# Combining the even layer's experts by matrix products with diagonal gates

## The chip, the cores and the metric

The kernel runs on one core of one Trainium2 chip. The metric is the device time of one execution in microseconds (us). Three runs of the kernel before gave 1182.02, 1181.76 and 1177.32 us; the median is 1181.76.

## What is computed

The reference is two consecutive layers of a hybrid backbone over 256 latent tokens and 256 context tokens of width 1024. Each layer has a mixer (the first, even one: state-space heads beside attention; the second, odd one: a matrix memory called mLSTM) and then a mixture of 16 experts, of which each token uses two. The change touches the end of the first layer's mixture and the beginning of the second layer:

```python
out = out + gates[..., e:e + 1] * (a @ w2[e])          # in moe: two of the 16 gates of a token are not zero
...
x_lat = x_lat + g_f * moe(h_lat, ...)                  # end of layer 0, latent stream
x_ctx = x_ctx + cg_f * moe(h_ctx, ...)                 # end of layer 0, context stream
...
h_lat = rmsnorm(x_lat, norm_mix[l]) * (1.0 + sc_m) + sh_m    # beginning of layer 1
h_ctx = rmsnorm(x_ctx, norm_mix[l]) * (1.0 + csc_m) + csh_m
```

So for each token the two expert outputs y0 and y1 are weighted by the token's two gates w0 and w1, the sum is multiplied by a row vector g, and the product is added to the residual stream x. Then x is normalised and modulated for the second layer.

## The kernel before, in words

The 512 tokens lie in four tiles of 128 (partitions are tokens): tiles 0 and 1 are the context (`CTX`), tiles 2 and 3 the latent stream (`LAT`). Each engine runs one hand-written list of steps in order (lines 2831 to 3012); semaphores tie the lists together, and a wait holds up everything behind it on its engine.

At the end of the first layer's mixture, GpSimd scatters expert outputs into a DRAM buffer (`ydram`), so that each token's two outputs lie side by side. When all are stored, SyncE issues four loads of 1 MB (line 2781) in the order tile 2, 3, 0, 1; each brings y0 and y1 of one tile into `ybuf(0, t)` and `ybuf(1, t)`. Behind these loads the same queue fetches the odd layer's input weights.

Meanwhile TensorE (PE) turns the modulation vectors g into rows (`pe_grow`, line 1312) and works out two chunks of the second layer's modulation (`COMB_MODS`: `pe_mod`, lines 423 and 429, with a copy by ScalarE at line 440 and a sum by VectorE at line 446).

The combination before is done by ScalarE and VectorE (DVE), tile by tile: ScalarE (ACT) scales y0 by w0 (`act_gate`, line 2792); VectorE takes y1 times w1 plus that (line 2799), times g (line 2800), plus x (line 2801). Then follows the normalisation: ScalarE sums the squares (line 512), VectorE and ScalarE work out the reciprocal root (lines 488 to 499), VectorE scales the tile (line 579), TensorE transposes it block by block (line 606), and ScalarE and VectorE write the modulated blocks out of PSUM into `hT` (lines 555 and 588).

The two latent tiles go first. Once their blocks of `hT` are written, TensorE starts the odd layer's input projection (`pe_in_odd`, line 1431). Its blocks are, in order, four query blocks that need only the latent half of `hT` (256 columns), then keys and values, which need both halves (512 columns). While the query blocks run, VectorE and ScalarE combine and normalise the context tiles. Before query block 3 TensorE transposes the context tiles (line 1448), and after it come the gates (`pe_gates`, line 673), which are the first product that needs the context's half of `hT`. An f32 product is written as one call of `pe.matmul` in the code and shows as two MATMUL instructions in the trace: eight calls of a query block are sixteen instructions.

Of the kernel before, what the change touches and what calls it, by code (L numbers as in the profile page):

```python
# [21 lines left out]
ACT = mybir.ActivationFunctionType  # L22
# [33 lines left out]
def lat(t):  # L56
    return t >= 2
# [7 lines left out]
def hybrid_program(nc, x, c, ctx, c_ctx, router_w, router_b, norm_mix, norm_ffn, w_mod, b_mod,  # L65
# [6 lines left out]
    def S(name):  # L72
        if name not in sems:
            sems[name] = nc.alloc_semaphore(name)
        return sems[name]
# [136 lines left out]
    def bank(b, n=512):  # L212
        return psum[:, b, 0:n]
# [76 lines left out]
    def dve_step(ins):  # L290

        ins.then_inc(S("dve_step"), 1)
        dve.wait_ge(*dve_more("dve_step"))
# [138 lines left out]
    def pe_mod(m):  # L432
        pe_mod_rows(m)
        pe_mod_cols(m)
# [61 lines left out]
    def act_rstd(n, a=0):  # L496
        v, y = stat2[:, 0, a:a + n], stat2[:, 1, a:a + n]
        act.wait_ge(*act_more("var_ready"))
        act.activation(y, v, ACT.Sqrt).then_inc(S("rstd_guess"), 1)
# [11 lines left out]
    def act_norm_sum(l, which, t):  # L511
        act.activation(turned_rows(l, which, t), xres[:, t, :], ACT.Square, accum_out=stat[:, t:t + 1]).then_inc(S("sum_ready"), 1)
# [918 lines left out]
    def pe_in_odd():  # L1431
        def transposes(j):
            kind, b = IN_ODD[j]
            pe.wait_ge(S("conv_done"), 6 + j + 1)
            bk = 4 + j % 2
            if j >= 6:
                pe.wait_ge(*pe_more("tok_done"))
            src = kTo[:, b, :] if kind == "k" else accv[:, j % 4, :]
            for t in range(NT):
                mm = pe.transpose(psum[:, bk, P * t:P * t + P], src[:, P * t:P * t + P], ident)  # L1440
            mm.then_inc(S("tok_full"), 1)

        at = None
        for j, (kind, b) in enumerate(IN_ODD):
            bk = (j + 2) % 4
            if j == 3:
                pe.wait_ge(S("mcol_done"), COMB_MODS[1] + 1)
                pe_norm_part(1, 0, CTX)
            if j == 4:
                pe_norm_end()  # L1450
                weights_here(OD0 + 1)
                w = slot(OD0 + 1, 32)
                pe_gates(6, [(w, H * q) for q in range(4)], (range(KD), range(KD))).then_inc(S("in_full"), 2)
            if j >= 4:
                pe.wait_ge(*pe_more("raw_ready"))
            pos = OD0 + 1 + j // 4 if j >= 4 else OD0
            if pos != at:
                weights_here(pos)
                at = pos
            w = slot(pos, 512)  # L1460
            tok = slice(STREAM, TOK) if kind == "q" else slice(0, TOK)
            for k in range(KD):
                mm = pe.matmul(bank(bk, tok.stop - tok.start), w[:, k, P * (b % 4):P * (b % 4) + P], hT[:, k, tok],  # L1463
                               start=k == 0, stop=k == KD - 1)
            mm.then_inc(S("in_full"), 1)
            if j >= 7:
                transposes(j - 3)
        for n in range(4):
            half, t = n // 2, 2 + n % 2
            pos = OD0 + 5 + half  # L1470
            if n % 2 == 0:
                weights_here(pos)
            pe.wait_ge(*pe_more("raw_ready"))
            w = slot(pos, 512)
            for k in range(KD):
                mm = pe.matmul(bank((18 + n) % 4), hT[:, k, P * t:P * t + P], w[:, k, :], start=k == 0, stop=k == KD - 1)  # L1476
            mm.then_inc(S("in_full"), 1)
            if n < 3:
                transposes(13 + n)
            if n == 2:  # L1480
                pe_ml_prepare()
        pe_ml_scores(3)
# [1191 lines left out]
    def ybuf(j, i):  # L2674
        return view(9216 + 1024 * (2 * i + j), [D])
# [111 lines left out]
        for half in ydram[1].rearrange("(h p a) n -> h p (a n)", h=2, p=P):  # L2787
            pool.dma_start(half, xres[:, 2:4, :].rearrange("p t n -> p (t n)")).then_inc(S("dram_zeroed"), 16)

    def act_gate(i):  # L2790
        act.wait_ge(*act_more(f"yback{i}", 16))
        act.activation(ybuf(0, i), ybuf(0, i), ACT.Copy, scale=gatew[:, i, 0:1]).then_inc(S("y1_scaled"), 1)

    def dve_combine(t):
        dve.wait_ge(S("grow_done"), GROW_AFTER[0][1])
        dve.wait_ge(*dve_more(f"yback{t}", 16))
        dve.wait_ge(*dve_more("y1_scaled"))
        y = ybuf(0, t)
        dve_step(dve.scalar_tensor_tensor(y, ybuf(1, t), gatew[:, t, 1:2], y, ALU.mult, ALU.add))
        dve_step(dve.tensor_tensor(y, y, grow_comb[0 if lat(t) else 1], ALU.mult))  # L2800
        dve.tensor_tensor(xres[:, t, :], xres[:, t, :], y, ALU.add).then_inc(S("comb_done"), 1)

    def act_combine():

        act_gate(2)
        act_gate(3)
        act_fetch(ACT.Sqrt)
        for n, t in enumerate(LAT):
            act.wait_ge(S("comb_done"), n + 1)
            act_norm_sum(1, 0, t)  # L2810
            act_rstd(1, t)
            act_gate(n)
        act_norm_rows(1, 0, 0)

    def dve_combine_all():

        for t in LAT:
            dve_combine(t)
        for t in LAT:
            dve_norm_scale(1, 0, [t])  # L2820
        dve_norm_rows(1, 0, 0)
        dve_odd_clear()
        for t in CTX:
            dve_combine(t)
        dve_norm_scale(1, 0, CTX)
        dve_norm_rows(1, 0, 1)

# [3 lines left out]
    with nc.Block() as block:  # L2831
# [41 lines left out]
        @block.scalar  # L2873
        def _(eng):
            act_setup()
            act_first_sums()
            act_mod(0)
            act_mod(1)
            act_first_rows(0)
            act_mod(2)  # L2880
            act_mod(3)
            act_first_rows(1)
            act.wait_ge(*act_more("raw_cleared"))
            act_in_even("xbc")
            act_setup_rest()
            act_conv()
            act_ssd_rows()
            act_in_even("kv", "q")
            act_rstd(10 * NT)
            act_in_even("z")  # L2890
            act_ssd_prepare()
            act_ssd()
            act_ssd_out()
            act_att_prepare()
            act_att()
            act_grow((0, 1), grow_out)
            act_out(0)
            act_router(0, ALL)
            act_moe(0)
            act_extra(0, ALL)  # L2900
            act.wait_ge(S("out_done"), 8)
            act_grow((0, 1), grow_comb)
            act_mod(COMB_MODS[0])
            act_mod(COMB_MODS[1])
            act_combine()
            act_in_odd()
            act_ml()
            act_ml_out()
            act.wait_ge(S("comb_done"), NT)
            act_grow((0,), grow_out)  # L2910
            act_out(1)
            act_router(1, LAT)
            act_moe(1)
            act_extra(1, LAT)

        @block.vector
        def _(eng):
            dve_setup()
            dve_norm_scale(0, 0, ALL)
            dve_mod(0)  # L2920
            dve_setup_rest()
            dve_mod(1)
            dve_first_bias(0)
            dve_first_acol(0)
            dve_first_rows(0)
            dve_mod(2)
            dve_mod(3)
            dve_first_bias(1)
            dve_first_acol(1)
            dve_first_rows(1)  # L2930
            dve_router_setup()
            dve_in_even()
            dve_ssd_rows()
            dve_qk_norm()
            dve_ssd_prepare()
            dve_ssd()
            dve_ssd_out()
            dve_att_prepare()
            dve_att()
            dve_mod_bias(0, FIRST, MODC)  # L2940
            dve_acol(0, 1)
            dve_out(0)
            dve_mod(NORM_MOD)
            dve_norm_rows(0, 1, 0)
            dve_mod(LIST_MODS[0])
            dve_router(0, ALL)
            dve_moe(0)
            dve_extra(0, ALL)
            dve_mod_bias(1, 0, 4)
            dve_acol(1, 0)  # L2950
            dve_mod(COMB_MODS[0])
            dve_mod(COMB_MODS[1])
            dve_combine_all()
            dve_mod_bias(1, 4, 8)
            dve_in_odd()
            dve_ml_prepare()
            dve_ml()
            dve_ml_out(OUT_ORDER[1])
            dve_mod_bias(1, 8, 10)
            dve_acol(1, 1)  # L2960
            dve_out(1)
            dve_norm_rows(1, 1, 0)
            dve_router(1, LAT)
            dve_moe(1)
            dve_last()
            dve_extra(1, LAT)

        @block.tensor
        def _(eng):
# [24 lines left out]
            pe_moe(0)  # L2994
            pe_extra(0, ALL)
            pe_grow(0, 1, (0, 1))
            for m in COMB_MODS:
                pe_mod(m)
            for t in LAT:
                pe_norm_part(1, 0, [t])  # L3000
            pe_norm_end()
# [85 lines left out]
```

## Time and profile before

| | |
|---|---|
| median of three runs | 1181.76 us (1177.32 to 1182.02) |
| the profiled execution's own time | 1179.53 us |
| its span, first to last instruction | 1177.9 us |
| TensorE busy | 1056.8 us |
| VectorE busy | 492.6 us |
| ScalarE busy | 257.6 us |
| mean granted TensorE clock | 0.967 of full speed |

The span is what the trace shows; the own time has 1.6 us more around it. Times in the trace count from the start of the span. The chain that ended last, followed back from the last instruction, is 73% TensorE and 11% VectorE. The stretch that the change touches lies between 638 and 690 us. Here a row of the timeline reads: start, duration, engine, line, operation, output<-input, shape, number of instructions merged, and in brackets the engine's idle time before it with what ended that.

### The profile page before, as it was taken

How to read it: one execution, taken by the hardware profiler on the slowest of the kernel's cores; microseconds unless marked ns; L12 is line 12 of the kernel's file. 1: busy time of each engine (PE TensorE's matmuls, PEld its weight loads, DVE VectorE, ACT ScalarE, POOL GpSimd, SP SyncE). 2: the span in 40 equal slices, each digit the busy share in tenths (PEclk: the TensorE clock that was granted, in tenths of full speed). 3: DMA queues.
4: the chain of work that ended last, by engine and by line, in shares of the span. 5: the costliest groups of instructions: out<-in, count | busy, mean ns of one | idle time of the engine just before them, and what ended most of it. 6: DMA issues, size and time to landing. Idle time of an engine off the chain costs nothing.

```text
span 1177.9 us, 14048 instructions
## 1 busy us (share of the span) xinstructions
PE 1056.8 (90%) x5369; PEld 548.6 (47%) x5369; DVE 492.6 (42%) x945; ACT 257.6 (22%) x531; POOL 206.9 (18%) x219
## 2 busy tenths in 40 slices
PE   3899989788998999999999598999858889989897
PEld 2346446444454454444454443445633555544442
DVE  2256569564034322222231769433852624322125
ACT  2123123475123000000011433114420211100001
POOL 0201023000110543133111000100001244441000
PEclk9999999999999999999999899899959789999999
DMA  9553239900619599999998952224338689999993
GB/s 342 176 199 142 71 134 326 379 20 8 278 46 384 182 380 420 417 419 416 368 424 309 344 177 71 72 72 150 137 151 324 278 323 417 409 415 418 426 416 122
DMA packets 72639, 311.00 MB, mean 264 GB/s; under 512 B 9772, under 2 KB 12008, under 8 KB 55147
## 3 DMA queue, kind: packets, MB, share of 16 engines
q1 hardware_dynamic: 61915, 291.07, 62.9%
q0 software_dynamic: 9776, 15.59, 3.9%
q10 hardware_dynamic: 864, 3.15, 0.7%
q8 instruction: 62, 1.02, 0.3%
q14 instruction: 22, 0.18, 0.0%
HBM read 306.83 MB, written 16.65 MB: 275 GB/s over the span
## 4 chain that ended last, share of the span: by engine, by line
PE 73%; DVE 11%; DMA 8%; ACT 4%; issue 2%; SPq 0%; POOL 0%; DVEq 0%; ACTq 0%
PE psum L2265 11%; PE psum L2268 9%; PE psum L1341 7%; DMA ring<-in_moe_w 7%; PE psum L700 6%; PE psum L2304 6%; PE psum L2299 5%; PE psum L1463 5%; PE psum L423 4%; PE psum L1476 2%; PE psum L631 2%; PE psum L1983 1%; PE psum L1010 1%; PE psum L692 1%; DMA ring<-in_w_mod 1%
## 5 line engine op out<-in xcount | busy, mean ns | idle before, releaser
L2426 POOL DMA_INDIRECT arena<-hdram,idxl x116 | 116.7, 1006 | 246.2 <-DVE arena L2367 154.0
L2380 DVE TENSOR_TENSOR arena<-arena,psum 128x512 f32<-128x512 f32 x32 | 22.0, 688 | 263.2 <-PE psum L2265 135.5
L1463 PE MATMUL psum<-arena,ring 128*128 128x512 f32 (+1 forms) x256 | 100.6, 550 | 1.3 <-ACT arena L555 1.3
L1341 PE MATMUL psum<-ring,arena 128*128 128x512 f32 x192 | 85.0, 603 | 1.5 <-ACT arena L1322 1.5
L2340 ACT ACTIVATE arena<-psum 128x512 f32<-128x512 f32 x32 | 19.1, 597 | 288.4 <-PE psum L2299 172.0
L2265 PE MATMUL psum<-arena 128*64 128x256 f32 x672 | 78.4, 391 | 2.3 <-issue 2.3
L1463 PEld LDWEIGHTS psum<-arena,ring 128*128 128x128 f32 x256 | 48.8, 194 | 47.2 <-issue 44.0
L2265 PE MATMUL psum<-ring,arena 128*64 128x256 f32 x608 | 68.6, 380 | 2.3 <-DMA ring<-in_moe_w 1.6
L2268 PE MATMUL psum<-arena 128*128 128x512 f32 x160 | 69.8, 593 | 0.8 <-DMA arena<-in_moe_w 0.8
L700 PE MATMUL psum<-ring,arena 128*128 128x512 f32 (+1 forms) x192 | 69.0, 522 | 0.0
L1375 POOL TENSOR_TENSOR wide<-wide,arena 128x512 f32<-128x512 f32 x12 | 15.2, 1265 | 305.6 <-DVE arena L1355 305.6
L423 PE MATMUL psum<-ring,spad 128*32 128x512 f32 x384 | 48.6, 627 | 17.9 <-DMA ring<-in_w_mod 12.6
L2268 PE MATMUL psum<-ring,arena 128*128 128x512 f32 x144 | 62.9, 593 | 0.7 <-DVE arena L2067 0.7
L2265 PEld LDWEIGHTS psum<-arena 128*64 128x64 f32 x672 | 50.3, 141 | 27.3 <-issue 6.0
L2367 DVE STREAM_TRANSPOSE arena<-arena 128x1024 f32<-128x1024 f32 x29 | 58.9, 2030 | 0.0
L1341 PEld LDWEIGHTS psum<-ring,arena 128*128 128x128 f32 x192 | 36.9, 194 | 47.0 <-issue 45.1
L2265 PEld LDWEIGHTS psum<-ring,arena 128*64 128x64 f32 x608 | 44.6, 137 | 23.2 <-DMA ring<-in_moe_w 2.5
L2374 DVE COPY arena<-psum 128x512 f32<-128x512 f32 x32 | 22.1, 692 | 79.0 <-PE psum L2304 44.4
L2299 PE MATMUL psum<-ring,arena 128*64 128x512 f32 x208 | 48.8, 612 | 5.7 <-DMA ring<-in_moe_w 4.7
L2349 ACT ACTIVATE arena<-psum 128x512 f32<-128x512 f32 x32 | 19.1, 597 | 153.6 <-PE psum L2265 85.3
L700 PEld LDWEIGHTS psum<-ring,arena 128*128 128x128 f32 x192 | 36.4, 190 | 32.6 <-issue 31.0
L2418 POOL DMA_INDIRECT ydram<-arena,idxl x30 | 30.4, 1014 | 119.5 <-DVE arena L2374 113.5
(427 smaller groups left out, 1487.5 us busy)
## 6 DMA issues: line engine op xcount, KB each, us to landing
ring<-in_moe_w SPq DMA_DIRECT2D x46, 2048.0 KB, 17.3
arena<-in_moe_w SPq DMA_DIRECT2D x45, 2048.0 KB, 17.2
ring<-in_w_mod SPq DMA_DIRECT2D x24, 2048.0 KB, 8.8
ring<-in_od_w_in SPq DMA_DIRECT2D x6, 2048.0 KB, 11.4
wide<-in_moe_w SPq DMA_DIRECT2D x5, 2048.0 KB, 28.7
ring<-in_ev_w_in SPq DMA_DIRECT2D x3, 2048.0 KB, 16.7
arena<-ydram SPq DMA_DIRECT2D x6, 1024.0 KB, 7.2
ring<-in_ev_w_out SPq DMA_DIRECT2D x2, 2048.0 KB, 9.4
```

The costliest lines, as they stand in the source:

```text
L423: mm = pe.matmul(psum[j:j + 32, mod_bank(m), :], spad[:, k, :], w[:, k, :], start=k < 4, stop=k >= 4)
L631: mm = pe.matmul(bank(b), w[:, k, P * b:P * b + P], hT[:, k, :], start=k == 0, stop=k == KD - 1)
L700: mm = pe.matmul(bank(bk, n), hT[:, k, P * b:P * b + P], w[:, k, :], start=k == 0, stop=k == KD - 1)
L1341: mm = pe.matmul(bank(out_bank(n)), catT[:, k, P * t:P * t + P], w[:, k, :], start=k == 0, stop=k == KD - 1)
L1463: mm = pe.matmul(bank(bk, tok.stop - tok.start), w[:, k, P * (b % 4):P * (b % 4) + P], hT[:, k, tok], start=k == 0, stop=k == KD - 1)
L2265: mm = pe.matmul(psum[64 * g:64 * g + 64, hbank(e, j), 0:256], xT[b][:, k, 0:64], w[:, k, 256 * g:256 * g + 256], start=k == 0, stop=k == ...
L2268: mm = pe.matmul(bank(hbank(e, j)), xT[b][:, k, :], w[:, k, :], start=k == 0, stop=k == KD - 1)
L2299: mm = pe.matmul(psum[64 * half:64 * half + 64, 2, :], aT[b][:, k % 2, 64 * (k // 2):64 * (k // 2) + 64], w[:, k, 512 * half:512 * half + ...
L2304: mm = pe.matmul(bank(2 + half), aT[b][:, k, :], w[:, k, 512 * half:512 * half + 512], start=k == 0, stop=k == KF - 1)
L2367: dve.transpose(xT[e % 2].rearrange("p k (g i) -> p g k i", g=4), xq[e % NX].rearrange("p (g j k) -> p g k j", g=4, k=KD)).then_inc(S("xt_ ...
L2418: return pool.indirect_dma_start(rows, bass.IndirectOffsetOnAxis(ap=col, axis=0), src, None, bounds_check=rows.shape[0] - 1, oob_is_err=False)
L2426: pool.indirect_dma_start(xq[e % NX][:, 256 * g:256 * g + 256], None, xrows(l), bass.IndirectOffsetOnAxis(ap=idxl[:, g, e:e + 1], axis=0), ...
```

## The change

The scaling by the two gates and their sum move from ScalarE and VectorE to TensorE: for each tile, VectorE writes two 128x128 matrices with w0 and w1 on the diagonal, and TensorE multiplies them with y0 and y1, both products adding up in PSUM. VectorE then takes the PSUM result times g and adds x. The latent products stand between the two modulation chunks on TensorE. The context's products stand in the odd layer's projection, before query blocks 1 and 2. The second modulation chunk's copy on ScalarE and its sum on VectorE move behind latent work. The diagonals lie in parts of `hT` that are not in use then; the products go to banks 2 to 7 of PSUM.

```diff
@@ pe_in_odd
             bk = (j + 2) % 4
+            if j in (1, 2):
+                pe.wait_ge(S("mcol_done"), COMB_MODS[1] + 1)
+                pe_combine(j - 1)
             if j == 3:
-                pe.wait_ge(S("mcol_done"), COMB_MODS[1] + 1)
                 pe_norm_part(1, 0, CTX)
@@ the combination
-    def act_gate(i):
-        act.wait_ge(*act_more(f"yback{i}", 16))
-        act.activation(ybuf(0, i), ybuf(0, i), ACT.Copy, scale=gatew[:, i, 0:1]).then_inc(S("y1_scaled"), 1)
-
-    def dve_combine(t):
+    dgate = [hT[:, 4:6, 0:STREAM].rearrange("p t (j n) -> p t j n", j=2), view(0, [2, 2, P])]
+    COMB_ORDER = (2, 3, 0, 1)
+    COMB_BANK = {2: 4, 3: 2, 0: 4, 1: 6}
+
+    def dve_gate_diagonals():
+
+        for t in COMB_ORDER:
+            for j in range(2):
+                last = dve.tensor_scalar(dgate[t // 2][:, t % 2, j, :], ident, gatew[:, t, j:j + 1], None, ALU.mult)
+            last.then_inc(S("diag_ready"), 1)
+
+    def pe_combine(t):
+
+        pe.wait_ge(S("diag_ready"), NT + COMB_ORDER.index(t) + 1)
+        pe.wait_ge(*pe_more(f"yback{t}", 16))
+        for half in range(2):
+            for j in range(2):
+                mm = pe.matmul(bank(COMB_BANK[t] + half), dgate[t // 2][:, t % 2, j, :], ybuf(j, t)[:, 512 * half:512 * half + 512],
+                               start=j == 0, stop=j == 1)
+        mm.then_inc(S("comb_full"), 1)
+
+    def dve_combine_products(t):
         dve.wait_ge(S("grow_done"), GROW_AFTER[0][1])
-        dve.wait_ge(*dve_more(f"yback{t}", 16))
-        dve.wait_ge(*dve_more("y1_scaled"))
+        dve.wait_ge(S("comb_full"), COMB_ORDER.index(t) + 1)
         y = ybuf(0, t)
-        dve_step(dve.scalar_tensor_tensor(y, ybuf(1, t), gatew[:, t, 1:2], y, ALU.mult, ALU.add))
-        dve_step(dve.tensor_tensor(y, y, grow_comb[0 if lat(t) else 1], ALU.mult))
+        dve_step(dve.tensor_tensor(y.rearrange("p (b n) -> p b n", b=2), psum[:, COMB_BANK[t]:COMB_BANK[t] + 2, :],
+                                   grow_comb[0 if lat(t) else 1].rearrange("p (b n) -> p b n", b=2), ALU.mult))
         dve.tensor_tensor(xres[:, t, :], xres[:, t, :], y, ALU.add).then_inc(S("comb_done"), 1)
 
     def act_combine():
 
-        act_gate(2)
-        act_gate(3)
+        for n in CTX:
+            act_more(f"yback{n}", 16)
+        act_mod(COMB_MODS[0])
         act_fetch(ACT.Sqrt)
         for n, t in enumerate(LAT):
             act.wait_ge(S("comb_done"), n + 1)
             act_norm_sum(1, 0, t)
+            if n == 0:
+                act_mod(COMB_MODS[1])
             act_rstd(1, t)
-            act_gate(n)
         act_norm_rows(1, 0, 0)
 
     def dve_combine_all():
 
+        for n in CTX:
+            dve_more(f"yback{n}", 16)
+        dve_gate_diagonals()
+        dve_mod(COMB_MODS[0])
         for t in LAT:
-            dve_combine(t)
+            dve_combine_products(t)
+        dve_mod(COMB_MODS[1])
         for t in LAT:
             dve_norm_scale(1, 0, [t])
         dve_norm_rows(1, 0, 0)
         dve_odd_clear()
         for t in CTX:
-            dve_combine(t)
+            dve_combine_products(t)
         dve_norm_scale(1, 0, CTX)
         dve_norm_rows(1, 0, 1)
@@ ScalarE's list: before act_combine()
-            act_mod(COMB_MODS[0])
-            act_mod(COMB_MODS[1])
@@ VectorE's list: before dve_combine_all()
-            dve_mod(COMB_MODS[0])
-            dve_mod(COMB_MODS[1])
@@ TensorE's list
             pe_grow(0, 1, (0, 1))
-            for m in COMB_MODS:
-                pe_mod(m)
+            pe_mod(COMB_MODS[0])
+            for t in LAT:
+                pe_combine(t)
+            pe_mod(COMB_MODS[1])
             for t in LAT:
                 pe_norm_part(1, 0, [t])
```

The loops over `CTX` with `act_more` and `dve_more` issue nothing: they only keep the engines' counts of `yback0` and `yback1`, which the second layer uses again.

## Rows read from the trace of the kernel before

**Rows 1.** The page: busy time and its share of the span by engine.

```profile
PE 1056.8 (90%) x5369; PEld 548.6 (47%) x5369; DVE 492.6 (42%) x945; ACT 257.6 (22%) x531; POOL 206.9 (18%) x219
```

**Rows 2.** Waits from 630 to 700 us: who waited, total us, times, longest us.

```profile
PE psum L606 <- DVE arena L579: 11.9, 3, 10.1
```

**Rows 3.** Timeline of PE from 634 to 745 us.

```profile
634.36 3.65 PE L2299 MATMUL psum<-ring,arena 128*64 128x512 f32 x16 [1.00 <-DVE arena L2386]
...
646.21 1.92 PE L423 MATMUL psum<-ring,spad 128*32 128x512 f32 x16 [0.28 <-DVE mcol L446]
648.85 0.66 PE L429 MATMUL psum<-cf,modrow 128*128 128x128 f32 x4 [0.72 <-ACT modrow L440]
...
662.10 1.92 PE L606 MATMUL psum<-cf,arena 128*128 128x128 f32 x8 [0.54 <-DVE arena L579]
665.33 10.60 PE L1463 MATMUL psum<-arena,ring 128*128 128x256 f32 x48 [1.31 <-ACT arena L555]
677.21 1.94 PE L606 MATMUL psum<-cf,arena 128*128 128x128 f32 x16 [1.29 <-DVE arena L579]
678.99 3.62 PE L1463 MATMUL psum<-arena,ring 128*128 128x256 f32 x16
...
689.52 27.73 PE L1463 MATMUL psum<-arena,ring 128*128 128x512 f32 x64
```

**Rows 4.** Timeline of DVE from 634 to 745 us.

```profile
645.96 0.19 DVE L446 TENSOR_REDUCE mcol<-psum 128x8 f32<-128x32 f32 x1 [6.17 <-PE psum L429]
...
651.29 1.22 DVE L2800 TENSOR_TENSOR arena<-arena 128x1024 f32<-128x1024 f32 x1
...
656.26 1.23 DVE L2801 TENSOR_TENSOR wide<-wide,arena 128x1024 f32<-128x1024 f32 x1
657.41 0.14 DVE L488 TENSOR_SCALAR stat<-stat 128x1 f32<-128x1 f32 x1
...
661.29 0.75 DVE L579 TENSOR_SCALAR arena<-wide,stat 128x1024 f32<-128x1024 f32 x1
...
671.68 1.22 DVE L2801 TENSOR_TENSOR wide<-wide,arena 128x1024 f32<-128x1024 f32 x1
```

**Rows 5.** The chain that ended last, around 658 us: start, us, what.

```profile
657.79 1.04 ACT arena L2792
```

**Rows 6.** Timeline of SP's queue: the four loads of expert outputs.

```profile
642.18 2.08 SPq L2781 DMA_DIRECT2D arena<-ydram  x4
```

**Rows 7.** Issues at 642.1 and at 642.6 us: size, us from issue to landing.

```profile
arena<-ydram SPq DMA_DIRECT2D x1, 1024.0 KB, 4.9
...
arena<-ydram SPq DMA_DIRECT2D x1, 1024.0 KB, 6.9
```

**Rows 8.** By line: for lines 2744 and 2768 ns min/median/max; else busy us, mean ns.

```profile
L2744 PE MATMUL psum<-arena,modrow x8: 592/592/667, 1168.8 to 1171.9; 128*128 128x512 f32 x8
...
L2768 DVE TENSOR_TENSOR arena<-psum,cb x4: 683/684/692, 1169.9 to 1173.9; 128x512 f32<-128x512 f32 x4
...
L2715 DVE TENSOR_SCALAR arena<-cb,rt 128x128 f32<-128x128 bf16 x8 | 2.4, 372 | 0.0
...
L1181 PE MATMUL psum<-cb 128*128 128x512 bf16 x16 | 4.8, 380 | 0.0
```

**Rows 9.** Timeline of PE: three stretches that follow idle time.

```profile
736.59 1.09 PE L1440 MATMUL psum<-cf,arena 128*128 128x128 f32 x4 [4.72 <-DVE arena L1555]
737.47 7.74 PE L1463 MATMUL psum<-arena,ring 128*128 128x512 f32 x12
...
1052.51 5.35 PE L2299 MATMUL psum<-ring,arena 128*64 128x512 f32 x16 [2.82 <-DMA ring<-in_moe_w]
```

**Rows 10.** Windows: us, busy by engine, granted PE clock, DMA share, GB/s.

```profile
1052.40:1058.00 5.60, 5.49 (x17) 1.67 (x18) 0.11 (x2) 0.09 (x1) 3.90 (x4) 0.70 1.02 428
...
960.00:1000.00 40.00, 38.27 (x271) 21.65 (x272) 11.80 (x12) 4.31 (x8) 14.66 (x15) 0.91 0.99 402
```

**Rows 11.** Waits of SP's queue from 860 to 960 us.

```profile
SPq L2521 <- DVE arena L1926: 41.9, 1, 41.9
```

## The prediction

> **What bounds the kernel now.** The page comes first: TensorE is busy for nine tenths of the span and every other engine for less than half [rows 1]. Work moved onto TensorE is therefore suspect, unless it lands where TensorE waits. The waits of the stretch show one such hole: TensorE waited 10.1 us for the first scaled latent tile [rows 2]. The timelines of TensorE and VectorE around it then tell what the stretch is made of [rows 3, 4]. Up to 662.10 it is a chain of VectorE and ScalarE (combine two latent tiles, normalise, scale), with TensorE idle. From 665.33 it is TensorE's: query blocks 0 to 2 run as 48 instructions in 10.60 us without a break, and the context's chain on VectorE and ScalarE is hidden under them but for 1.29 us of idle time before the context's transposes at 677.21 [rows 3]. The reader should see that the two halves differ: before 665 TensorE has room, after it there is hardly any. The change puts two tiles' products in the first half and two in the second.
>
> **What one product costs.** A tile's combination is four calls of 128x128 by 128x512 in f32. The nearest row is line 2744, the same kind of product: four calls show as eight instructions [rows 8]. In a long run such instructions follow each other every 27.73 / 64 = 0.433 us [rows 3], so a tile takes 8 x 0.433 = 3.47 us. From the first start of line 2744 at 1168.8 to its last at 1171.9 it is 3.1 us for seven steps, which gives the same.
>
> By the Trainium skill (VectorE: DVE Perf Modes, the section on the TRN2 errata) a matmul takes 6 cycles plus its columns at 2.4 GHz, which would be an estimated 0.216 us a call and 0.86 us a tile. The trace disagrees for f32: a call is two instructions of 0.433 us.
>
> **The latent half, step by step.** *Diagonals:* eight small VectorE instructions, at most 0.37 us each by the nearest row, line 2715 [rows 8], and not below nothing. That is at most 3.0 us, in the 6.17 us for which VectorE idles before line 446 at 645.96 [rows 4]; I cost them at nothing. Without that cover they would cost those 3.0 us. The added wait for the diagonals on TensorE falls away with it.
>
> *Products:* TensorE is free at about 645.95. Tile 2's data were issued at 642.18 and landed 4.9 us later, so at 647.1 [rows 6, 7]. This is the new wait; behind it on TensorE stand both products and the second modulation chunk. Tile 3's landed 6.9 us after an issue at about 642.6, at 649.5, in time. So the products run from 647.1 to 650.6 and on to 654.0.
>
> *VectorE:* a product with g out of PSUM, 128x1024, has no row. From above it is twice line 2768, 2 x 0.684 = 1.37 us, from below line 2800 out of SBUF, 1.22 us [rows 4, 8]; I take 1.24 with the issue, as 1024 columns out of SBUF are nearest in length. With the addition (1.23) a tile takes 2.5 us, so tile 2 is done at 653.1 and tile 3 at 656.55. Before, tile 3 was done at 657.49 [rows 4].
>
> *The modulation chunk moved behind:* line 423 takes 1.92 us, from 654.0 to 656.0; ScalarE's copy takes 0.7 us (line 423 ended at 648.13 and line 429 began at 648.85), line 429 0.66 us [rows 3], the sum on VectorE 0.2 us: done at 657.6. It is now what is late: line 488, behind it on VectorE, starts at 657.6 where it started at 657.41 [rows 4]. The odd weights on SyncE's queue that wait for a ring place of this chunk move by the same 6 us, but are values' weights, wanted after the keys; I cost that at nothing.
>
> *ScalarE:* the context's gating of 1.04 us stood in the chain between tile 2's root and tile 3's squares [rows 5]. It goes, but tile 3's line 488 can't start before VectorE has scaled tile 2, 2.13 us after its line 488, at 659.75; line 579 follows 1.4 us later, at 661.15 instead of 661.29. So the latent half gains 0.15 us: the removed VectorE work is eaten by the landing and by the modulation chunk.
>
> **The context half.** From the start of query block 0 TensorE now has block 0, product, block 1, product: 2 x 3.5 (10.60 / 3, [rows 3]) + 2 x 3.47 = 13.9 us. Only then can VectorE finish tile 1: 2.5 us, to 16.4. From the end of line 2801 (671.68 + 1.22) to the transposes at 677.21 it took 4.3 us [rows 3, 4], and nothing in that chain of squares, root and scaling changes: 20.7 us. Before, it was 677.21 - 665.33 = 11.9. So **the context's transposes come 8.8 us later**, and with them block 3 and the gates; TensorE has block 2 to put into that wait and then idles 3.3 us where it idled 1.29. VectorE's removed instruction (1.28 us a tile) is no gain here, as VectorE now waits for the product. GpSimd's clearing of the second layer's buffers, which waits for the last tile, moves too and is wanted far later.
>
> **The clock.** TensorE's granted clock has two levels, 2.4 and 1.2 GHz. After 1.29 us of idle time it was the higher one: 16 transposes in 1.94 us at 677.21, against 8 in 1.92 us at 662.10 after the long idle time [rows 3]. After 2.82 us it was partly the lower one: a mean of 0.70, and 16 instructions of line 2299 took 5.35 us, where 16 of the same form took 3.65 at 634.36: 1.7 us lost [rows 3, 9, 10]. After 4.72 us 12 instructions took 7.74 us instead of 12 x 0.433 = 5.2, and four transposes 1.09 instead of 0.49: 3.1 us lost [rows 9]. The new idle time of 3.3 us is nearest to 2.82, so I add 1.7 us, with 0 and 3.1 as ends. In the latent half TensorE idles about 2.4 us before tile 2's transposes, also nearest to 2.82, so the transposes stay at the level at which they are now: nothing. Ends: 0.9 us gained if the eight transposes run at the higher level, 1.7 us lost if block 0 runs wholly at the lower.
>
> **The sum.** -0.15 + 8.8 + 1.7 = 10.35 us. What follows (gates, their long VectorE chain, keys, values, the memory, the second mixture) hangs on block 3 and the gates, and I find no slack in it. On the profiled execution's own time of 1179.53 (span 1177.9 and 1.6 around it) that gives **1189.9 us**. This execution lies 2.2 us under the median of the three runs and 2.2 above their lowest.
>
> **The rivals.**
>
> *Cheap products (not slower).* Place: TensorE; mechanism: a diagonal product runs as one instruction a call rather than two. The bf16 row of line 1181 gives 4.8 / 16 = 0.30 us for it [rows 8], so 1.2 us a tile. Then the context costs 2 x 3.5 + 2 x 1.2 + 2.5 + 4.3 = 16.2, so 4.3 us more, and the modulation chunk is through at 654.2 instead of 657.41, 3.2 us less: 1.1 us in all, 1180.6 us, up to 1182.5 with the clock's loss. It decides from about 2.3 us a tile: below that the total is under 5.9 us. Against it: every f32 row here, line 2744 above all. The rule cited above on a matmul's cycles is this rival taken further. Chance 0.06.
>
> *A hidden delay.* The second layer's expert weights keep the DMA engines at 0.99 [rows 10], so a later odd layer might vanish under that stream: 1179.5 to 1182 us. Against it: the stream's first loads waited 41.9 us for VectorE's line 1926 of the odd layer [rows 11], so the stream starts later by the same amount. It would need loads that run ahead of the odd layer, and I see none. Chance 0.06.
>
> *The clock falls twice, for long.* Block 0 at the lower level (1.7) and 3.1 rather than 1.7 us lost at the context: 1179.53 + 8.8 - 0.15 + 1.7 + 3.1 = 1193.0 us. For it: the clock stayed low through 12 instructions after 4.72 us; against: the idle times are shorter here. Chance 0.15.
>
> *A shorter latent half*, with data that land 1.1 us sooner than here, 0.9 us of clock gained and none lost at the context: 1179.53 + 8.8 - 0.15 - 2.0 = 1186.2 us. It is the low end of the forecast, not a case of its own.
>
> **How the numbers follow.** The forecast has 0.70, the long fall of the clock 0.15, cheap products 0.06, the hidden delay 0.06, and 0.03 is left for a gain that I have not seen. Half a per cent, 5.9 us, is about what a measurement of this kernel can tell from no change. The forecast and the clock's rival are slower by more than that in nearly all their width; 0.04 of them I give to no change, as a median may move by 2 us. So slower 0.81, same 0.15, faster 0.04. The range runs from 1186.2 less 2.2 for the run, rounded down to 1183.5, up to 1193.0 plus 2.2, so 1195.5; it leaves out the two rivals that end lower and little else.
>
> **What the profile after would show.** Right: products of 3.4 to 3.7 us a tile, the first starting near 647.1; line 488 near 657.6; tile 3's transposes near 662; query blocks and products alternating, and the context's transposes some 20.7 us after block 0 starts, with about 3.3 us of idle time and a lower clock before or in them; the gates 8 to 11 us later than before, and every later stage moved by the same. Wrong: a product near 1 us; tile 3's line 579 more than 2 us earlier than 661.29; the context's transposes within 5 us of where they were; or a later stage that takes the delay back.

## The result, and the profile after

The changed kernel took 1191.41 us (median of ten runs, 1185.6 to 1194.8) against 1179.17 for the kernel before (ten runs): a ratio of 1.0089, interval 1.0072 to 1.0105, so 8.5 to 12.4 us slower. Measured again beside the experiments it was 1188.07 against 1180.02, ratio 1.0066 (1.0045 to 1.0087). Forecast: 1189.9, in a range of 1183.5 to 1195.5, slower.

The profiled execution after is one of the two shortest of the ten: own time 1185.71, span 1184.1. Its touched stretch starts 2.8 us later in the trace (line 1312 at 640.74, before at 637.95), ahead of all that the change touches. Read the times below as distances from that point, or from query block 0 of the projection (block 0 from here on). Line numbers move by two: the projection, line 1463 before, is 1465; the products are line 2809, VectorE's two steps 2817 and 2819.

TensorE's timeline, which answers to [rows 3]:

```profile
640.74 3.96 PE L1312 MATMUL psum<-cf,mcol 128*128 128x128 f32 x32
...
650.08 7.11 PE L2809 MATMUL psum<-arena 128*128 128x512 f32 x16 [1.37 <-DMA arena<-ydram]
657.12 1.92 PE L423 MATMUL psum<-ring,spad 128*32 128x512 f32 x16
659.76 0.66 PE L429 MATMUL psum<-cf,modrow 128*128 128x128 f32 x4 [0.72 <-ACT modrow L440]
662.75 1.80 PE L606 MATMUL psum<-cf,arena 128*128 128x128 f32 x8 [2.34 <-DVE arena L579]
664.81 1.84 PE L606 MATMUL psum<-cf,arena 128*128 128x128 f32 x8 [0.26 <-DVE arena L579]
668.04 3.69 PE L1465 MATMUL psum<-arena,ring 128*128 128x256 f32 x16 [1.39 <-ACT arena L555]
671.57 3.60 PE L2809 MATMUL psum<-arena 128*128 128x512 f32 x8
675.00 3.62 PE L1465 MATMUL psum<-arena,ring 128*128 128x256 f32 x16
678.45 3.60 PE L2809 MATMUL psum<-arena 128*128 128x512 f32 x8
681.89 3.62 PE L1465 MATMUL psum<-arena,ring 128*128 128x256 f32 x16
688.85 1.97 PE L606 MATMUL psum<-cf,arena 128*128 128x128 f32 x16 [3.35 <-DVE arena L579]
690.66 3.62 PE L1465 MATMUL psum<-arena,ring 128*128 128x256 f32 x16
694.21 6.20 PE L673 MATMUL psum<-arena,ring 128*8 128x512 f32 x56
```

The 10 us hole is filled but for waits of 1.37 and 2.34 us, and yet block 0 starts 27.30 us after line 1312, where it was 27.38 (665.33 - 637.95). Then the alternation shows: block, product, block, product, block, and 3.35 us of waiting. The context's transposes come 20.81 us after block 0 starts, where they came 11.88 us after it. The gates start 53.47 us after line 1312, before 44.59: 8.9 us later.

VectorE's timeline, which answers to [rows 4]:

```profile
642.50 1.76 DVE L2800 TENSOR_SCALAR arena<-cf,gatew 128x128 f32<-128x128 f32 x8
...
653.86 1.23 DVE L2817 TENSOR_TENSOR arena<-psum,arena 128x1024 f32<-128x1024 f32 x1 [4.92 <-PE psum L2809]
...
658.55 1.23 DVE L2819 TENSOR_TENSOR wide<-wide,arena 128x1024 f32<-128x1024 f32 x1
660.45 0.19 DVE L446 TENSOR_REDUCE mcol<-psum 128x8 f32<-128x32 f32 x1 [0.67 <-PE psum L429]
660.56 0.14 DVE L488 TENSOR_SCALAR stat<-stat 128x1 f32<-128x1 f32 x1
...
664.00 0.75 DVE L579 TENSOR_SCALAR arena<-wide,stat 128x1024 f32<-128x1024 f32 x1
...
675.27 1.23 DVE L2817 TENSOR_TENSOR arena<-psum,arena 128x1024 f32<-128x1024 f32 x1 [7.17 <-PE psum L2809]
...
682.16 1.23 DVE L2817 TENSOR_TENSOR arena<-psum,arena 128x1024 f32<-128x1024 f32 x1 [4.40 <-PE psum L2809]
```

The last two rows carry the finding: VectorE, whose own chain set the context's pace before, now sits idle for 7.17 and 4.40 us until TensorE has come round to the product. The work left VectorE; the wait stayed.

### The profile page after: what moved, and what is told of

It is laid out like the page before. It is cut to its first block, busy times and chain, and to the rows that moved or that the text cites. A ratio compares the mean times of both kernels' runs of the same rounds, so it can differ in the third digit from the quotient of the medians.

```text
span 1184.1 us, 14101 instructions
## 1 busy us (share of the span) xinstructions
PE 1063.6 (90%) x5387; PEld 553.4 (47%) x5401; DVE 489.2 (41%) x949; ACT 253.2 (21%) x527; POOL 206.9 (17%) x219
## 4 chain that ended last, share of the span: by engine, by line
PE 75%; DVE 10%; DMA 8%; ACT 4%; issue 2%; SPq 0%; POOL 0%; DVEq 0%; POOLq 0%; ACTq 0%
PE psum L2270 11%; PE psum L2267 10%; PE psum L1341 7%; PE psum L700 6%; PE psum L1465 6%; PE psum L2301 5%; PE psum L2306 5%; DMA arena<-in_moe_w 3%; PE psum L423 3%; DMA ring<-in_moe_w 3%; PE psum L1478 2%; PE psum L631 2%; PE psum L1985 1%; PE psum L1010 1%; PE psum L2809 1%
## 5 line engine op out<-in xcount | busy, mean ns | idle before, releaser
L2267 PE MATMUL psum<-arena 128*64 128x256 f32 x672 | 75.5, 381 | 2.2 <-issue 2.2
```

The costliest lines, as they stand in the source:

```text
L2267: mm = pe.matmul(psum[64 * g:64 * g + 64, hbank(e, j), 0:256], xT[b][:, k, 0:64], w[:, k, 256 * g:256 * g + 256], start=k == 0, stop=k == ...
```

## The experiments

Ratios are against the kernel before, measured on the same chip in the same session; 0.001 is 1.2 us, and the interval behind a ratio is the 95% one. A claim on a single stretch comes from one profile of each run. The edits are shortened, mostly to TensorE's lines; where a half goes back to ScalarE and VectorE, its old steps (`act_gate`, `dve_combine`) come back with it. The clock is read from the granted levels and from the length of block 0 (sixteen instructions: 3.69 us at the higher level, 6.44 to 6.50 at a mean granted clock of 0.56).

**One half undone each time.** In the first run the context tiles return to ScalarE and VectorE, in the second the latent ones.

```diff
-            if j in (1, 2):                      # first run: no product in the query blocks
-                pe_combine(j - 1)
...
         for t in CTX:
-            dve_combine_products(t)
+            dve_combine(t)                       # with act_gate(n) back behind act_rstd(1, t)
```

> The latent tiles stay products on TensorE, the context tiles go back to ScalarE and VectorE. Theory 'cover' (the context's products stand in front of query blocks that had no room for them): the context's transposes come 12 us after query block 0 starts, as before, and the time is that of the kernel before within 1.5 us (ratio 0.999 to 1.001). Rival 'latent half' (the delay comes from the wait for tile 2's data and from the second modulation chunk's later place): most of the 10.5 us stays, 1186 us or more.

Measured: 0.9989 (0.9972 to 1.0006). Block 0 came 27.6 us after line 1312. The time is that of the kernel before, as the cover theory has it, but the distance is not: the context's transposes came 14.01 us after block 0, where I expected 12, since blocks 0 to 2 ran partly at the lower clock and took 12.97 us, before 10.60:

```profile
672.18 12.97 PE L1463 MATMUL psum<-arena,ring 128*128 128x256 f32 x48 [1.26 <-ACT arena L555]
686.19 1.94 PE L606 MATMUL psum<-cf,arena 128*128 128x128 f32 x16 [1.03 <-DVE arena L579]
```

```diff
-            pe_mod(COMB_MODS[0])                 # second run: latent tiles as before
-            for t in LAT:
-                pe_combine(t)
-            pe_mod(COMB_MODS[1])
+            for m in COMB_MODS:
+                pe_mod(m)
```

> The latent tiles go back to ScalarE and VectorE, the context's products stay between the query blocks. Cover: the transposes of the context come 20.7 us after block 0 starts, and the time is that of the changed kernel within 1.5 us, 8 to 11 us above the kernel before. Rival latent half: close to the kernel before, under 1183 us.

Measured: 1.0052 (1.0035 to 1.0070). The distance from block 0 to the context's transposes is 690.40 - 669.58 = 20.82 us:

```profile
669.58 3.69 PE L1465 MATMUL psum<-arena,ring 128*128 128x256 f32 x16 [1.25 <-ACT arena L555]
673.11 3.60 PE L2809 MATMUL psum<-arena 128*128 128x512 f32 x8
...
690.40 1.97 PE L606 MATMUL psum<-cf,arena 128*128 128x128 f32 x16 [3.35 <-DVE arena L579]
```

So the slowdown belongs to the context's half, and the latent half alone is no loss. The rival of the latent half falls. But 1.0052 is 6.1 us (4.1 to 8.3), less than the 8 to 11 that I expected of it, and the two halves add up to 4.8 us, where the changed kernel lost 10.5 in one session and 7.8 (5.3 to 10.3) in another. The changed kernel was not measured beside these two runs, so it is not shown that the halves fail to add up; the later runs ask what else enters.

**Both context products behind block 0.**

```diff
-            if j in (1, 2):
+            if j == 1:
                 pe.wait_ge(S("mcol_done"), COMB_MODS[1] + 1)
-                pe_combine(j - 1)
+                for t in CTX:
+                    pe_combine(t)
```

> Both context products stand behind block 0, so that blocks 1 and 2 cover the chain behind tile 1's product. Cover: the last product ends 10.4 us after block 0 starts, the transposes come 17.2 to 17.5 us after it with no idle time of TensorE over 0.5 us, 3.3 us sooner than in the changed kernel; the time is 5 to 7 us above the kernel before. Rival 'sum of work' (the time goes by TensorE's added 6.9 us wherever in the query blocks they stand): like the changed kernel, 9 to 11 us above.

Measured: 1.0033 (1.0016 to 1.0049), 3.9 us. The direction is that of the cover theory: the same added work costs less when blocks 1 and 2 stand behind it. As the changed kernel was not measured beside this run, the distance is the firmer sign. It was 21.17 us, but here block 0 took 6.46 us at the lower clock; at 3.69 it would have been 18.4. The changed kernel has 23.55 with block 0 at the lower clock (its second profile, below) and 20.81 at the higher: 2.4 us more either way, where 3.3 were expected. TensorE idled 0.93 us, more than expected, and ScalarE's timeline shows why:

```profile
681.94 0.39 ACT L1509 ACTIVATE arena<-psum 128x256 f32<-128x256 f32 x1 [3.15 <-PE psum L1466]
682.23 1.05 ACT L512 ACTIVATE arena<-wide 128x1024 f32<-128x1024 f32 x1
```

Tile 1 was combined at 681.04, but its squares (line 512) stand in ScalarE's list behind the copy of block 1 (line 1509), which waits for that block to end.

**Filling the idle time to hold the clock.** Products that nobody reads, in the idle time before the context's transposes (first run), in the latent half (second), in both (third). Between the first and the others the changed kernel itself was taken again.

```diff
                 pe_combine(j - 1)                # the context's filler
             if j == 3:
+                for k in range(7):
+                    pe.matmul(bank(1, STREAM), w[:, k, 0:P], hT[:, k, STREAM:TOK], start=True, stop=True)
                 pe_norm_part(1, 0, CTX)
...
             pe_mod(COMB_MODS[1])                 # the latent filler; a like one of 640 columns before pe_norm_end()
+            pe.matmul(bank(6), ident, cf[:, 0:512], start=True, stop=True)
+            pe.matmul(bank(6), ident, cf[:, 0:512], start=True, stop=True)
+            pe.matmul(bank(6, STREAM), ident, cf[:, 0:STREAM], start=True, stop=True)
```

> The changed kernel with 14 more instructions of a query block's kind (3.0 us, into a bank that block 3 overwrites) in TensorE's 3.35 us of idle time before the context's transposes; they add nothing to the result. Cover, with the clock as a term of its own: the transposes come no later than in the changed kernel (20.7 to 21.0 us after block 0), and the time is 1 to 2 us below the changed kernel's, as the clock no longer falls in some executions. Rival 'no clock' (the idle time never costs clock): the same time as the changed kernel, 10 to 11 us above the kernel before.

> The changed kernel itself, for a comparison on the chip of the next three runs: 1.007 to 1.011 of the kernel before. Query block 0 takes 3.5 or 6.5 us, by whether the clock is still low from the idle time before it.

> The changed kernel with about 3.2 us of idle products of constants (into bank 6, written again before it is read) in TensorE's two idle stretches of the latent half, behind the second modulation chunk and behind the latent transposes. Theory 'low clock in block 0': the clock stays at its higher level, block 0 takes 3.5 us instead of up to 6.5, the context's transposes still come 20.7 us after it starts; the time falls by 2 to 4 us against the changed kernel. Rival 'no clock': the same time as the changed kernel.

> Both fillers (this latent one and that of the context's idle time). Low clock: no lower level between 645 and 700 us, what is left is the delay by the place alone, so 6 to 9 us above the kernel before, and 2 to 5 us below the changed kernel. No clock: like the changed kernel.

Measured: the context's filler 1.0049 (1.0032 to 1.0066), the changed kernel again 1.0066, the latent filler 1.0065 (1.0047 to 1.0083), both 1.0050 (1.0027 to 1.0074). In time that is inconclusive: the intervals overlap, and the first filler ran in another session than the rest. The traces say more. This is TensorE's timeline of the changed kernel's second profile:

```profile
665.03 6.44 PE L1465 MATMUL psum<-arena,ring 128*128 128x256 f32 x16 [1.26 <-ACT arena L555]
...
688.58 3.68 PE L606 MATMUL psum<-cf,arena 128*128 128x128 f32 x16 [3.35 <-DVE arena L579]
692.05 4.82 PE L1465 MATMUL psum<-arena,ring 128*128 128x256 f32 x16
```

and its windows over these two stretches (length, busy times, then granted clock, DMA share, GB/s):

```profile
665.00:671.40 6.40, 6.37 (x17) 5.21 (x18) 0.07 (x1) 0.00 (x0) 0.00 (x0) 0.56 0.90 333
688.50:692.10 3.60, 3.52 (x17) 3.52 (x18) 1.02 (x3) 1.25 (x3) 0.00 (x0) 0.50 0.79 312
```

The same kernel, nearly the same idle times as in the profile after (1.26 and 1.39 us before block 0, 3.35 in both before the transposes), and two losses that the profile after lacks: 2.75 us in block 0, and about 2.9 us (1.7 in the transposes, 1.2 in block 3) after the 3.35 us of idle time. In the profile after, too, the clock was low in the latent transposes (a mean of 0.57 from 662.7 to 666.7), but it was back up when block 0 began. With both fillers neither loss occurs: block 0 in 3.69 us, the transposes in 1.97. With the latent one alone block 0 takes 3.69 us and the transposes 3.67:

```profile
667.49 3.69 PE L1465 MATMUL psum<-arena,ring 128*128 128x256 f32 x16 [0.60 <-ACT arena L555]
...
688.31 3.67 PE L606 MATMUL psum<-cf,arena 128*128 128x128 f32 x16 [3.35 <-DVE arena L579]
```

With the context's filler alone block 0 took 6.50 us and the transposes 1.97. So each idle time can cost clock, in some executions and not in others. Each filler stands in two profiles, and its loss occurs in neither. That it removes the loss is likely but not shown: without the context's filler, two of four profiles with the 3.35 us of idle time had fast transposes all the same, and without the latent one, one of five with the latent products (the profile after) had a fast block 0. That the median hardly moves asks what the later stages do.

**The delay alone.** The kernel before, with idle products between block 2 and the context's transposes; the combination is untouched. The second run has 14 instead of 12.

```diff
             if j == 3:
                 pe.wait_ge(S("mcol_done"), COMB_MODS[1] + 1)
+                for k in range(12):
+                    pe.matmul(bank(1), ident, cf[:, 0:512], start=True, stop=True)
                 pe_norm_part(1, 0, CTX)
```

> The kernel before with 10.4 us of idle products of constants on TensorE between query block 2 and the context's transposes, which add nothing to the result; the combination is as before. The transposes then come 20.9 us after block 0 starts, as in the changed kernel, with no idle time of TensorE and nothing else changed. Theory 'rigid': everything behind moves by 9.0 us, so the time is 8 to 10 us above the kernel before. Rival 'given back': the later stages run with less of the lower clock when they start later, so the delay arrives as 5 to 7 us.

> The same with 12.1 us of idle products, so 10.7 us later than before. Rigid: 1.7 us above the run with 10.4 us of them. Given back, by where the later stages fall in the clock's own time: any value between the same time and 3 us more; less than it would speak for a clock that follows the start of a stage.

Measured: 1.0056 (1.0036 to 1.0077), 6.6 us, and 1.0116 (1.0094 to 1.0138), 13.7 us. The distances were 20.74 and 22.45 us, as meant:

```profile
667.55 10.60 PE L1465 MATMUL psum<-arena,ring 128*128 128x256 f32 x48 [1.44 <-ACT arena L555]
677.99 10.46 PE L1449 MATMUL psum<-cf 128*128 128x512 f32 x24
688.29 1.91 PE L606 MATMUL psum<-cf,arena 128*128 128x128 f32 x16
```

The first of them matches the profile after stage by stage: 53.41 us from line 1312 to the gates (after 53.47), 245.4 from there to the second mixture (245.4), 244.7 to the end (244.5). So later transposes alone, with the combination as before, reproduce the profile after.

1.7 us more of delay cost 7.1 us more at the median of five and six runs: neither theory had that. The first run's interval, 4.2 to 9.1 us, holds what both theories forecast for it. The two profiles show one way in which such a difference arises. Both reach the output projection, line 1341, at 888.5; from there to the first expert product is 50.5 us in the one and 53.6 in the other. The rows of line 1341, the shorter delay first, and the windows of that stretch:

```profile
888.50 27.70 PE L1341 MATMUL psum<-ring,arena 128*128 128x512 f32 x64 [0.73 <-ACT arena L1322]
```

```profile
888.50:939.00 50.50, 40.12 (x194) 20.41 (x194) 17.88 (x58) 10.29 (x19) 5.06 (x4) 0.93 0.85 347
```

```profile
888.53 29.47 PE L1341 MATMUL psum<-ring,arena 128*128 128x512 f32 x64 [0.73 <-ACT arena L1322]
```

```profile
888.50:942.10 53.60, 44.76 (x193) 22.78 (x193) 17.61 (x56) 10.52 (x20) 5.06 (x4) 0.84 0.80 329
```

Same work, granted clock 0.93 against 0.84. It is also the difference between the profile after and the one before, in the whole stretch from the gates to the second mixture. After:

```profile
694.20:939.60 245.40, 210.88 (x1014) 111.06 (x1017) 131.52 (x298) 69.33 (x163) 12.24 (x12) 0.94 0.42 159
```

and before:

```profile
682.50:932.30 249.80, 217.38 (x1016) 113.68 (x1016) 131.35 (x296) 69.40 (x163) 12.24 (x12) 0.91 0.41 156
```

That is 4.4 us shorter on work that the change doesn't touch: TensorE is busy 6.5 us less at a clock of 0.94 instead of 0.91, VectorE and ScalarE the same. But no delay is needed for it. Two executions of one kernel, the first and the last run of the next group, differ in the same stretch by the same amount:

```profile
681.70:931.40 249.70, 216.70 (x1014) 113.72 (x1018) 131.24 (x297) 69.45 (x163) 12.24 (x12) 0.92 0.41 156
682.60:928.00 245.40, 210.90 (x1012) 110.85 (x1015) 131.50 (x297) 69.26 (x163) 12.24 (x12) 0.94 0.42 159
```

The changed kernel, too, has 245.4 us there in its first profile and 248.8 in its second. So this difference is one between executions, and no profile shows that the delay brings it about. From the second mixture to the end it is 244.5 us after and 245.6 before, and 244.8 and 245.7 in the two executions of the one kernel: nothing shows that the expert weights' stream absorbs the delay.

**The context's products in the hole.** The latent tiles on ScalarE and VectorE as before, and the context's products in the 10 us for which TensorE has nothing to do.

```diff
-            pe_mod(COMB_MODS[0])
-            for t in LAT:
-                pe_combine(t)
-            pe_mod(COMB_MODS[1])
+            for m in COMB_MODS:
+                pe_mod(m)
+            pe.wait_ge(S("mcol_done"), COMB_MODS[1] + 1)
+            for t in CTX:
+                pe_combine(t)
             for t in LAT:
                 pe_norm_part(1, 0, [t])
@@ pe_in_odd
-            if j in (1, 2):
-                pe.wait_ge(S("mcol_done"), COMB_MODS[1] + 1)
-                pe_combine(j - 1)
```

> The latent tiles on ScalarE and VectorE as before; the context's products moved to TensorE's 10 us of idle time ahead of the latent transposes. Cover: the products cost nothing there, VectorE has one instruction less for each context tile, ScalarE's two gatings go, and TensorE's clock stays high through the latent transposes; the context's transposes come 10.5 us after block 0 starts (before 11.9), block 0 starts 0.5 to 1.5 us earlier; the time is 1.5 to 4 us below the kernel before. Rival 'sum of work': 6.9 us more of TensorE's time make it slower than the kernel before.

> The kernel with the context's products in the idle time ahead of the latent transposes, and 1.7 us of idle products of constants in the 2.6 us for which TensorE waits for the first context tile's data. Low clock: no lower level before block 0, which with blocks 1 and 2 takes 10.5 us instead of 12.05; 0 to 1.5 us below the kernel without them. No clock: the same time.

> The kernel with the context's products in the idle time ahead of the latent transposes, once more, since the last run with idle products in it came out no faster than the kernel before. Cover: the context's transposes 13.0 us or less after block 0, block 0 within 27 us of line 1312's first instruction, and a ratio of 0.996 to 0.9995 as before. Rival 'by the clock's phase': the first ratio was luck, and this one lies at 1.000 to 1.002.

Measured: 0.9979 (0.9963 to 0.9994), with 1.7 us of idle products 1.0012 (0.9998 to 1.0026), once more without them 0.9973 (0.9957 to 0.9989). It is the one version faster than the kernel before, by 2.5 us (0.7 to 4.4) and 3.2 us (1.3 to 5.1) in two sessions. The rival 'sum of work' falls: the same products that cost 6.1 us between the query blocks cost nothing here. TensorE's timeline of the last run:

```profile
653.54 8.80 PE L2806 MATMUL psum<-arena 128*128 128x512 f32 x16 [2.72 <-DMA arena<-ydram]
662.18 1.91 PE L606 MATMUL psum<-cf,arena 128*128 128x128 f32 x16
665.77 10.60 PE L1462 MATMUL psum<-arena,ring 128*128 128x256 f32 x48 [1.68 <-ACT arena L555]
677.30 1.97 PE L606 MATMUL psum<-cf,arena 128*128 128x128 f32 x16 [0.94 <-DVE arena L579]
```

Block 0 starts 26.50 us after line 1312 (639.27), 0.9 sooner than before, and the transposes follow 11.53 us later (12.98 in the first run of this kernel, where blocks 0 to 2 took 12.05 us). I expected 10.5; ScalarE's queue holds tile 1's squares behind block 1's copy here too, so VectorE waits, as its row in the first run of this kernel shows:

```profile
673.46 0.17 DVE L488 TENSOR_SCALAR stat<-stat 128x2 f32<-128x2 f32 x1 [5.17 <-ACT arena L512]
```

From line 1312 to the gates it is 44.80 us in the first run and 43.38 in the last, before 44.59. So the touched stretch shows at most 1.2 us of the gain; where the rest comes from is open.

The filler failed. It shortened the wait for the context's data to 0.90 us, but blocks 0 to 2 took 12.02 us, as in the first run without it (12.05) and unlike the second (10.60): it did not hold the clock. Its touched stretch is as long as in the first run (44.79 us to the gates), so why the kernel then came out slower than the one without the filler, in another session, stays open.

## Why the prediction was right, and where it was not

**The context half** carried it. 8.8 us were forecast from two products and a chain that starts only behind the second; 8.9 were measured (20.81 less the 11.88 of before; in the second profile 23.55, less the 2.75 that block 0 lost in clock, less 11.88). A product's row is 3.60 us long, and the next block starts 3.43 us after it (671.57 to 675.00). VectorE's step out of PSUM took 1.23 us, the lower end of my bounds, and not more than the same step out of SBUF. The delay alone, with the combination as before, gave the same distance and the same later stages.

The rule cited before on a matmul's cycles, from the Trainium skill (VectorE: DVE Perf Modes, the section on the TRN2 errata), would have made a tile's product 0.86 us as an estimate; the rows of line 2809 disagree, with 3.60 us. The same section's table charges a VectorE instruction 62 cycles more for a source in PSUM than in SBUF, an estimated 0.06 us; the trace disagrees there too, 1.23 us (line 2817, one of its two sources in PSUM) against 1.22 (line 2800 before, both in SBUF).

**The latent half** was right to a tenth: block 0 was forecast 0.15 us earlier at an unchanged clock, and came 0.08 earlier. Line 488, held by the modulation chunk, came 19.82 us after line 1312, before 19.46, so 0.4 later (0.2 forecast). The data landed 5.0 us after the issue, the diagonals took 1.76 us in idle time.

**The clock** was mis-sized. I added 1.7 us at the context's idle time, with 0 and 3.1 as ends, and nothing at block 0, with 1.7 as the worst. The first stayed within its ends: 0 in one profile, 2.9 in the other. The second was bounded wrongly: a block of 3.5 us at half the clock loses up to 3.5, not 1.7, and 2.75 was measured. So the two profiles lose 0 and 5.6 us where the sum has 1.7. That the median of the ten runs lies 10.5 us above the kernel before, against 10.35 in the sum, is in part luck; six later runs gave 7.8.

**"I find no slack in it"** is not settled. The later stages hang on the gates, as I said, but their length is not fixed: 249.8 us before, 245.4 after, at another granted clock. That is no slack that the delay uses up, as one kernel has both lengths in two executions. The delays alone moved the transposes by 8.9 and 10.6 us, and arrived as 6.6 us (4.2 to 9.1) and 13.7 us (11.1 to 16.3): the first less, the second more. The prediction has no term for such differences between executions, only 2.2 us of its range for the choice of the run. What decides between the lengths is open.

**The rivals.** Cheap products: refuted by line 2809. A hidden delay under the weights' stream: refuted by the time, 8.5 to 12.4 us longer, and the stream's stage is within 1.1 us of its length before. The long fall of the clock: it did occur, in the second profile (stretch up to the gates 14.4 us longer, of which some 5.6 clock). Its time of 1191.88 us lies near the forecast of 1193.0; it is one execution of several.

## What to carry to other kernels

Moving work to another engine paid here only where that engine waits: the context's products alone cost 6.1 us between the query blocks, and with them in the hole, some 16 us earlier, the kernel came out 2 to 3 us faster than before. In a chain of engines, look at who waits for the moved step: VectorE's saved instruction was worth nothing between the query blocks, because its input now came behind one. And two executions of one program differ here by 4 us in stages that no edit touches, at another granted clock; so judge a change of a few microseconds by several runs and by the touched stretch in the trace.

## What I had not expected of the hardware

By TensorE's clock the same program, with nearly the same idle times, loses 5.6 us in block 0 and around the context's transposes in one execution and nothing there in another: 16 transposes after 3.35 us of idle time took 1.97 us in the profile after and 3.68 in the next one. And 1.7 us of added idle products lengthened the kernel by 7.1 us at the median of a few runs; how much of that is the products' doing is open.
